# Stick-breaking attention with one reset scan, two softmax attentions taken in pairs of heads, and a re-timed HGRN2 stage: what it does to a 16-stage transformer kernel

## The reference, cut to what matters

```python
# na and mla: 16 heads each, softmax over 256 keys
s = jnp.where(col_mask[:, None, :], s + bias, NEG_INF)      # na only
p = jax.nn.softmax(s, axis=-1)
o = einsum('bhqk,bkhd->bqhd', p, v)                          # d = 64

# stick-breaking: 8 heads of 128, query blocks of 128 rows, keys up to the block's end
z = einsum('bqhd,bkhd->bhqk', q_blk, k_p) * scale
mask = k_pos[None, :] < q_pos[:, None]
log_beta = log_sigmoid(z)
log_1m = where(mask, log_sigmoid(-z), 0.0)
suffix = cumsum(log_1m, axis=3, reverse=True) - log_1m
w = where(mask, exp(log_beta + suffix), 0.0)
o = einsum('bhqk,bkhd->bqhd', w, v_p)
```

## Time and profile before

| what | value |
|---|---|
| median of 3 runs | 3063.12 us (3058.28 to 3063.68) |
| the profiled execution: its own time | 3055.57 us |
| its span, first to last instruction | 3053.8 us |
| PE busy | 2855.1 us, 93% |
| DVE busy | 2002.9 us, 66% |
| ACT busy | 1426.9 us, 47% |
| POOL busy | 98.7 us, 3% |

### The profile page before, as it was taken

One profiled execution on the slowest core, in us unless ns is written; L12 is line 12 of the kernel. 1 busy time (PEld: TensorE's weight loads), 2 busy tenths in 40 slices (PEclk: granted clock), 3 DMA queues, 4 the chain that ended last, 5 costly groups with the idle time before them and its releaser, 6 DMA issues.

```text
span 3053.8 us, 46734 instructions
## 1 busy us (share of the span) xinstructions
PE 2855.1 (93%) x19701; PEld 2639.7 (86%) x19701; DVE 2002.9 (66%) x2615; ACT 1426.9 (47%) x1904; POOL 98.7 (3%) x148
## 2 busy tenths in 40 slices
PE   7999979999988999999999999997999699896998
PEld 6999869999975999998799999996999599794897
DVE  5667766565657666557665665776656677746777
ACT  4445544444444544445554444554444444453443
POOL 0000000000002000001100000000000100000000
PEclk9999999999999999999999999998999899997999
DMA  7654326675541565553256566432664456442562
GB/s 227 188 161 138 112 82 215 186 207 186 159 145 49 184 184 183 182 167 93 94 181 186 166 200 186 132 125 69 199 185 154 138 173 200 152 156 65 166 192 98
DMA packets 404726, 478.41 MB, mean 157 GB/s; under 512 B 16555, under 2 KB 331653, under 8 KB 404517
## 3 DMA queue, kind: packets, MB, share of 16 engines
q1 hardware_dynamic: 400944, 467.33, 48.8%
q0 software_dynamic: 1776, 6.77, 0.8%
q10 hardware_dynamic: 1796, 1.33, 0.1%
HBM read 474.32 MB, written 1.05 MB: 156 GB/s over the span
## 4 chain that ended last, share of the span: by engine, by line
PE 82%; DVE 10%; ACT 4%; issue 3%; ACTq 0%; DVEq 0%
PE Wk L621 17%; PE Wk L623 16%; PE Wk L622 16%; PE Y L621 9%; PE Y L622 9%; PE Y L623 9%; DVE w_lo L1747 2%; DVE work L1986 1%; ACT w_hi L1246 1%; PE Y L971 1%; PE Y L874 1%; PE Y L726 1%; PE Wk L944 1%; PE Wk L960 0%; PE Wk L874 0%
## 5 line engine op out<-in xcount | busy, mean ns | idle before, releaser
L1747 DVE TENSOR_TENSOR w_lo<-ring,w_hi 128x1024 fp32r<-128x1024 f32 (+2 forms) x910 | 1070.4, 1200 | 690.1 <-ACT w_hi L1246 643.7
L621 PE MATMUL Wk<-xT_hi,w_hi 128*128 128x256 f32 x4320 | 1233.3, 285 | 21.0 <-DVE xT_lo L1786 17.7
L623 PE MATMUL Wk<-xT_hi,w_lo 128*128 128x256 f32 x4320 | 1225.6, 284 | 0.0
L622 PE MATMUL Wk<-xT_lo,w_hi 128*128 128x256 f32 x4320 | 1225.6, 284 | 0.0
L1246 ACT ACTIVATE w_hi<-ring 128x1024 fp32r<-128x1024 f32 (+1 forms) x894 | 906.8, 1039 | 645.0 <-PE Wk L623 431.7
L621 PEld LDWEIGHTS Wk<-xT_hi,w_hi 128*128 128x128 f32 x4320 | 832.2, 193 | 28.2 <-issue 14.8
L622 PEld LDWEIGHTS Wk<-xT_lo,w_hi 128*128 128x128 f32 x4320 | 832.4, 193 | 4.7 <-issue 0.9
L623 PEld LDWEIGHTS Wk<-xT_hi,w_lo 128*128 128x128 f32 x4320 | 831.9, 193 | 0.0
L621 PE MATMUL Y<-w_hi,hid_hi 128*128 128x512 f32 x904 | 353.5, 391 | 4.3 <-DVE hid_lo L1840 4.3
L622 PE MATMUL Y<-w_lo,hid_hi 128*128 128x512 f32 x904 | 352.1, 389 | 0.0
L623 PE MATMUL Y<-w_hi,hid_lo 128*128 128x512 f32 x904 | 350.9, 388 | 0.0
(11 more groups left out here) (283 smaller groups left out, 2829.1 us busy)
## 6 DMA issues: line engine op xcount, KB each, us to landing
ring<-in_ffn_w_gu SPq DMA_DIRECT2D x352, 512.0 KB, 4.4
ring<-in_ffn_w_down SPq DMA_DIRECT2D x224, 512.0 KB, 4.4
ring<-in_ffn_w_up SPq DMA_DIRECT2D x96, 512.0 KB, 5.9
ring<-in_hg_w_in SPq DMA_DIRECT2D x80, 512.0 KB, 3.6
ring<-in_na_w_in SPq DMA_DIRECT2D x24, 512.0 KB, 4.5
ring<-in_hg_w_out SPq DMA_DIRECT2D x16, 512.0 KB, 3.6
ring<-in_lru_w_in SPq DMA_DIRECT2D x16, 512.0 KB, 4.4
ring<-in_kv_w SPq DMA_DIRECT2D x16, 512.0 KB, 4.5
```

Source lines behind the costliest of these rows:

```text
L621: pe.matmul(o, l_hi, r_hi, start=first, stop=False)
L622: pe.matmul(o, l_hi, r_lo, start=False, stop=False)
L623: return pe.matmul(o, l_lo, r_hi, start=False, stop=last)
L1747: ins = dve.tensor_tensor(l, r, h.bitcast(F32), ALU.subtract)
```

## The change

- **stick.** The scores of query block 0 are made against its own 128 keys only, so a head has 128 + 256 = 384 elements in a partition instead of 512. The weight is written as exp(z minus a sum of softplus(z) over the later keys and the key itself). DVE needs three operations of 384 for it: softplus (line 2432 after), one scan whose multiplier is 0 where a row's sum starts anew (2433), and z minus the sum (2434). Only the two 128x128 diagonal blocks are masked, in one operation (2441). The scale is applied when q is saved. The scores of four heads, their logarithms and most of their weights are computed between the four value products.
- **na and mla.** Both use one `softmax_attention`. PE takes two heads in one round, with the matmuls of the two heads alternating (scores and values). The scaling by the inverse sum is moved: DVE makes two 128x128 diagonal matrices (`inv_diag`), and the turn to the other layout becomes a float32 matmul with them in place of a transpose. The maximum is negated by the reduction itself. The scores of the first two heads are made before the last products. The `flip` products of na are gone: the queries are stored backwards instead, and so is the output in `xT`.
- **w_out of the attentions** starts when the banks of its first half are free.
- **hg.** Within a pair, the splitting of the next weight unit is placed before the norm's work on ACT and before `save_z` and `save_q` on DVE. Pairs 0 and 1 are split into `hid_hi` and `hid_lo`, which are idle here, one level after another, and `pair_out` runs at levels 0, 2, 4 and 6. The units of the last pair are split later. Three units of the following stage are split at the end of the level loop, and DVE no longer splits units between the last output product and the residual.

The core of the diff:

```diff
+A_BANKS = (0, 1, 6, 7)
-MS_BANKS = (4, 4, 4, 2)
+MS_BANKS = (4, 4, 0, 2)
+HALVES_LAST = (0, 0, 1, 1, 2, 2, 3, 4, 5)
...
             def w_out(s, t0):
                 for j in range(2):
-                    t_product(*out_of(t0, j), first=j == 0)
+                    if j == 0:
+                        for n in range(2):
+                            pe.wait_ge(s_saved, saves_before(s) + 7 + n)
+                            y_half(out_of(t0, j), n, first=True)
+                    else:
+                        t_product(*out_of(t0, j), first=j == 0)
...
-                        if last and 3 <= i < 7:
-                            pair_out((i - 3) // 2, (i - 3) % 2)
+                        if last and i in (0, 2, 4, 6):
+                            pair_out(i // 2 % 2, i // 4)
...
+            def scores_of_pair(g, q_of, k_of):
+                for tt in range(TT):
+                    for h in (2 * g, 2 * g + 1):
+                        mm = pe.matmul(bank(A_BANKS[h % 4])[:, tt * T:(tt + 1) * T],
+                                       q_of(h)[:, tt * P:(tt + 1) * P], k_of(h), start=True, stop=True)
+                        if tt:
+                            mm.then_inc(s_psum, 1)
...
+                            mm = pe.matmul(bank(2 + h % 2)[:, kk * T + tt * P:kk * T + (tt + 1) * P],
+                                           at_p[:, h % 4, tt, kk * P:(kk + 1) * P], inv_diag[:, h % 2, tt, :],
+                                           start=True, stop=True)
...
+                for g in range(pairs + 2):
+                    if 1 <= g < pairs:
+                        scores_of_pair(g, q_of, k_of)
+                    if g >= 2:
+                        values(g - 2)
+                    if 1 <= g <= pairs:
+                        turned(2 * g - 2)
+                        turned(2 * g - 1)
...
-                    flip(i - 1)
-                pe.wait_ge(na_flipped, NA_H // 2)
...
+                turned(0)
+                for i in range(ST_H):
+                    if i + 1 < ST_H:
+                        turned(i + 1)
+                    if i + 4 < ST_H:
+                        scores(i + 4)
+                    values(i)
...
+                        if last and i == 1:
+                            squares_of(p_ - 1)
...
+                        if not last:
+                            ahead(HALVES_AHEAD + 10 * (p_ + 1) + i, s)
...
+                        else:
+                            ahead(HALVES_AHEAD + 38 + HALVES_LAST[i], s)
+                ahead(10 * HG_PAIRS + 10, s, over=True)
...
+                for i in range(1, NA_H + 4):
+                    if 2 <= i < NA_H:
+                        scores(i)
+                    if i <= NA_H:
+                        inverse_sums(i - 1)
+                    if i >= 5 and i % 2:
+                        g = (i - 5) // 2
+                        dve.wait_ge(s_out, h0 + 2 * g + 2)
+                        o = bank(4 + g % 2)[:, 0:T].rearrange("p (a t) -> p a t", a=split)
+                        split_out(g, 1, o, (s_high, g0 + g + 1), s_saved)
...
+                    step(dve.scalar_tensor_tensor(l, z, 0.0, l, ALU.max, ALU.add))
+                    step(dve.tensor_tensor_scan(sums_[:, ::-1], runs[:, ::-1], l[:, ::-1], 0.0, ALU.mult, ALU.add))
+                    dve.tensor_tensor(sums_, z, sums_, ALU.subtract).then_inc(t_sfx, 1)
...
-                splits(end[s] + 1)
+                if kind != "hg":
+                    splits(end[s] + 1)
```

442 lines of the change are left out of this document (242 added, 200 removed).

## The result

| what | before | after |
|---|---|---|
| median of the runs | 3063.40 us (3058.28 to 3063.80) | 2967.83 us (2963.30 to 2968.85) |
| ratio of the runs | | 0.9689, 95% interval 0.9672 to 0.9706 |
| the profiled execution: its own time | 3055.57 us | 2968.85 us |
| its span | 3053.8 us | 2967.0 us |
| PE busy | 2855.1 us, 93% | 2815.5 us, 95% |

The change is 95.6 us faster by the medians (3063.40 - 2967.83), and 86.8 by the two spans. The 8.8 between the two are explained further down.

A forecast was written before the change was run, and what follows sets the result against it. DVE was taken to bound stick and na, PE mla and dense stages, with 29.3 us idle per hg stage. Gains 25.5 + 21 + 8 + 39 = 93.5 gave 2962, plus 7.5 to the median: 2969 us, range 2943 to 3003.

The forecast's parts named there:

- The DVE prices: Stick: DVE's work per head falls from 6.3 to 3.4 us, 3.5 with waits; DVE sets the pace.
- the chain of turns: Stick: a stretch over 28 us would mean turns and copies, not DVE, set it at the low clock.
- 27.2 less 1.0 and 1: Stick: stretch gain 27.2, less 1.0 for scores among the products and one for the low clock; given as -25.5.
- the rival: na: the contention goes, the 128-wide scaling ending before POOL starts; a pair 4.95, 10.5 less, near 2958; chance 0.07.
- The clock's 1.4: na: PE has 3.9 of work in a 6.45 pair, so the clock may sit at half level: +1.4.
- the start and tail save about 7: mla: first scores and exponentials are made before the last product ends; 1.9 goes back for scores among the queries.
- (a): hg, pairs 0 to 2: the split ahead of save_z spends the waits where PE has other work: -8 a stage.
- (b): hg, last pair: 42.00 us becomes 31, each level's chain having PE work beside it: -10, allowing for the clock.
- (c): hg, end of stage: next stage's units are split earlier, removing PE's 2.1 wait before the residual: -1.5.
- my rival: The hg chain absorbs its gain, splits waiting for ACT's copy: each stage gains 9, total 2990 to 3000; chance 0.15.
- The halves: Rival: halves of the array don't overlap; mla 5.4 a pair, na hidden under DVE, about 5 more, 2974; chance 0.05.
- The slow side: Rival: slower than before, as low clock left by shortened stretches reaches dense products; decides from 94 us on; chance 0.03.

The follow-up runs named there:

- Run 9: The kernel before the change, run once more with a profile: 3064.07 us, its profiled execution 3063.98 us.
- Run 7: The changed kernel with scores, logarithms and sums of two stick heads instead of four made between the value products: 2991.93 us.
- run 8: The changed kernel with three stick heads instead of four made ahead, otherwise in its own order: 2977.09 us.
- run 6: The changed kernel with plain transposes for the diagonal-matrix products in na and mla, leaving the inverse-sum scaling out of the result: 2963.78 us.
- run 5: The changed kernel with scores and values of a pair's two heads one head after the other instead of alternating: 2967.00 us.
- Run 1: The changed kernel with hg's weight split in pairs 0 to 2 again behind the norm's work on ACT and save_z, save_q on DVE: 2991.03 us.
- run 2: The changed kernel with hg's last-pair output products at levels 3 to 6 again and the later units' splits as late as that needs: 2962.25 us.
- run 10: The changed kernel with hg's four last-pair output products halved, one part at each of levels 0 to 7: 2961.07 us.
- run 12: The changed kernel with halved output products at levels 0 to 7, later last-pair splits, and na's POOL mask addition after DVE's scalings: 2947.72 us.
- Run 4: The changed kernel with four instead of three units of the following stage split at the end of the hg level loop: 2967.97 us.
- Run 3: The changed kernel with POOL's mask addition in na waiting until DVE's two scalings of head h-3 are done: 2957.20 us.

## Why the prediction was right, point by point

**The total.** 2969 was forecast and 2967.83 measured, inside the range. That it is so close is partly luck. The sum from the profiled execution was 93.5, and the two traces differ by 86.8. The 6.7 too much was made up by the other step: I kept the 7.5 between the profiled execution and the median, and the runs after have nearly none (their own profiled one is 1.0 above their median). Run 9 showed why: the first trace of before was of an execution with less time at the half clock. From that run's 3063.98 the change is 95.1. The parts below are told apart by the stretches of the traces; runs undo the order inside hg's pairs, the places and splits of its last pair, the early stick heads and the diagonal product, and no run undoes the removal of the flips, the reset scan or the early first half of `w_out`.

**Stick, right (-24.5 for -25.5), for a reason that was half right.** The DVE prices held: 0.56, 0.96, 0.56, 0.41 and 0.84 are 3.3 a head, for 3.4 in the sum, and 24.8 of stretch for 23. But that DVE's work per head sets the stretch is only true with the four early heads and the order that comes with them. Run 7 took all of the gain away with that (163.3) and run 8 half (150.6), at the same arithmetic. I named the chain of turns as something that would show in a stretch over 28; I didn't price it. How much the early heads would gain with the old arithmetic, or the new arithmetic in the old order, no run shows, so the 24.5 can't be divided between the two. A slip in the sum: 27.2 less 1.0 and 1 is 25.2, not 25.5.

**na, right in sign and mechanism, 3.8 too small.** The pair of 6.41 for 6.45 and the scaling that keeps POOL's length are as forecast, against the rival. Mis-sized were the start and tail of the attention: from the last value product to `w_out` it is 48.5 where I had 50.4 + 1.4 for the clock, and the products end 11.3 earlier where I had 10.8. The clock's 1.4 didn't come, at 0.93 in that stretch; run 6, where the tail ran at 0.50, shows that it can.

**mla, 4.7 too large.** A pair is 4.73 for 4.6: the turns 1.89 for 1.76 and the scores 1.82 for 1.72. The step that failed is "the start and tail save about 7". What was won at the first exponentials (a wait of 3.2 before the first turn) went again at the second pair's scores: PE has nothing for 0.8 there, waiting for DVE at the last queries, and then the scores take 3.3 at a clock of 0.53, where they are 1.82 elsewhere. The stage's PE-bound part, from the first turn to `w_out`, went from 39.6 to 35.9, 3.7 less, and the stage gained 3.3. That halves overlap was right (1.08 for two heads); that consecutive ones hardly do was wrong (run 5): the 1.84 held a wait for ACT's copy.

**hg, -37.0 for -39, with three terms that were off.** (a) Pairs 0 to 2 gained 11.7 a stage, not 8: 7.2 in PE's idle time (10.8 before, 3.7 after), near the forecast, and 4.5 in busy time, at a clock of 1.00 against 0.97, which I had left out. Run 1 gives 11.1 and 11.5 of it back by the order alone. (b) The last pair with the border gained 7.7 and 10.5, and the ffn stage behind it lost 2.3, where I had 11.5 in all. The waits of 6.1 and 5.1 went, as forecast. But the step "`pair_out` now runs at levels 0, 2, 4, 6, so the chain of each level has PE work beside it" was wrong: four products cover four of eight chains at most, and the one at level 0 covers a chain that had PE work already. The last pair kept 10.1 us of idle PE, and run 2 took 3.4 off in each stage with other places and later splits, run 10 took 3.8 to 4.0 off with half products and the splits as they were, and run 12, with both, has 6.7 as run 2. What took the two long waits away, the norm's earlier chain or the later splits, no run tells apart. (c) The -1.5 at the end of the stage was a wait that changed its place: 2.1 before the residual became 0.3 there and 1.7 for `w_lo` in the stage behind, and the ffn stage is 2.3 longer. Run 4 moved it back and gained nothing. A part of my rival, that splits brought forward wait elsewhere, is true here.

**The rivals.** The hg chain did not absorb the gain. The contention didn't go by itself. The halves overlap. The slow side didn't come; but the argument that the low clock stays inside its stage was too strong, since run 9 shows 1.5 us of it behind each hg stage and 2.9 in a cffn stage.

By the Trainium skill (SBUF — State Buffer, section “SBUF: two separate sides”) VectorE and GpSimd lock a shared pair of ports for a whole instruction, and only some operations of VectorE want it. Run 3 agrees in both halves: the scaling waits for POOL (1.38 against 0.48), while the reduction, the cast and the addition beside the same POOL instruction keep their 0.69, 0.42 and 0.68.

## What to carry to other kernels

Where work goes round over three engines, follow the ring through the three programs before pricing an operation: what stands ahead of item n on each queue says how many items share one round, and a well-priced gain can hang on that. Work of the idle engine that is as long as the gap covers it; twice as long covers no second gap, and a piece is lost where the gap was covered already. A split moved out of one chain has to stand somewhere, and must not stand directly ahead of the next one's first operation. And before a sum is taken from one trace, look at its granted clock against a second one: here it was worth 8.4 us.

## What the runs showed of the hardware that was not expected

- Two float32 products on different halves of the array's columns take 1.08 together, as one alone, whether their matmuls alternate or not.
- Taking 6.2 us of work from PE in a stretch of 40.35 us that DVE bounds left the stretch as it was, but the tail behind it, which goes through PE, ran at a granted clock of 0.50 instead of 1.00, and the stage grew by 2.5 us. This is one trace of each kernel.
- Two executions of one kernel differ by 8.4 us of span (3053.8 and 3062.2) with the same instructions, at clocks of 0.969 and 0.966; most of it lay in dense stages (1.5 behind each hg stage, 2.9 in a cffn stage), where a stretch at the half clock had come to lie behind the border: the first 6.4 us of an ffn stage had 0.73 instead of 1.00.
